# Rotary pairs on GpSimd, norm sums in two parts, high-part products first and a retention product in three float32r passes, in a two-block transformer forward pass

## The reference, cut to what matters

```python
def rmsnorm(x, g):
    y = xf * rsqrt(mean(xf * xf, -1) + 1e-6)
def apply_rope_2(x, cos, sin):            # attention of the second model, heads of 128
    x1, x2 = split(x, 2, -1)
    return x * cos + concatenate([-x2, x1], -1) * sin
# retention, per head: scores (256 queries x 512 keys), with decay, times v (512 keys x 512)
y = einsum('bhij,bhje->bhie', scores, vc) + (q * q_dec) @ state
```

## Time and profile before

| | before |
|---|---|
| median of 3 runs (lowest, highest) | 3224.12 us (3220.11, 3224.12) |
| the profiled execution | 3224.9 us, its span 3223.1 us |
| PE busy | 3185.1 us, 99% of the span |
| PE weight loads busy | 2734.2 us, 85% |
| DVE busy | 2377.3 us, 74% |
| ACT busy | 1337.1 us, 41% |
| POOL busy | 640.2 us, 20% |
| mean memory traffic | 157 GB/s |

### The profile page before, as it was taken

The page is one execution under the profiler, slowest core; times in us unless marked ns, Lnnn a source line. Parts: engine busy times, 40 slices in busy tenths (PEclk is TensorE's granted clock), DMA queues, the critical chain, the costliest instruction groups (busy, mean ns, idle before and its releaser), DMA issues.

```text
span 3223.1 us, 46716 instructions
## 1 busy us (share of the span) xinstructions
PE 3185.1 (99%) x17344; PEld 2734.2 (85%) x17344; DVE 2377.3 (74%) x3055; ACT 1337.1 (41%) x1907; POOL 640.2 (20%) x526
## 2 busy tenths in 40 slices
PE   8999999999999999999999999999999999999999
PEld 4888888888888888888888898799888889789988
DVE  4878957868787635455768887966888896975887
ACT  3222233212232224333536456455645446555643
POOL 2212322202321131001323230100223231100122
PEclk9999999999999999999999999999999999999999
DMA  6655524646365433334665665445666665444665
GB/s 225 206 161 171 162 59 134 206 139 190 90 196 178 136 103 88 98 105 138 197 178 167 197 182 159 125 137 144 184 193 177 196 189 164 124 138 119 195 196 150
DMA packets 783677, 507.50 MB, mean 157 GB/s; under 512 B 15108, under 2 KB 737104, under 8 KB 783504
## 3 DMA queue, kind: packets, MB, share of 16 engines
q1 hardware_dynamic: 782336, 503.51, 52.9%
q0 software_dynamic: 368, 1.38, 0.1%
q10 hardware_dynamic: 800, 0.24, 0.0%
HBM read 504.01 MB, written 1.05 MB: 157 GB/s over the span
## 4 chain that ended last, share of the span: by engine, by line
PE 54%; DVE 5%; issue 1%; ACT 1%; DVEq 0%; ACTq 0%
PE bank L673 18%; PE bank L671 10%; PE bank L675 4%; PE bank L677 4%; PE bank L676 4%; PE bank L690 2%; PE bank L692 2%; PE bank L691 2%; PE bank L670 2%; DVE wlo_all L1605 2%; PE bank L1146 1%; PE bank L1011 1%; DVE g_ps L2104 0%; PE bank L978 0%; DVE xn_two L1703 0%
## 5 line engine op out<-in xcount | busy, mean ns | idle before, releaser
L1605 DVE TENSOR_TENSOR wlo_all<-raw,whi_all 128x1024 fp32r<-128x1024 f32 (+3 forms) x768 | 1005.7, 1312 | 443.8 <-ACT whi_all L1215 441.1
L1215 ACT CAST whi_all<-raw 128x1024 fp32r<-128x1024 f32 (+3 forms) x768 | 834.6, 1091 | 1041.8 <-PE bank L677 552.3
L675 PE MATMUL bank<-xn_two,whi_all 128*128 128x512 f32 (+1 forms) x1760 | 631.6, 359 | 3.2 <-DVE xn_two L1779 3.1
L677 PE MATMUL bank<-xn_two,wlo_all 128*128 128x512 f32 (+1 forms) x1760 | 624.2, 355 | 0.0
L676 PE MATMUL bank<-xn_two,whi_all 128*128 128x512 f32 (+1 forms) x1760 | 624.0, 355 | 0.0
L673 PE MATMUL bank<-xn_two,whi_all 128*128 128x512 f32 x1540 | 549.4, 396 | 0.0
L2247 POOL CAST h_two<-silu_g 128x256 f32 (+1 forms) x176 | 210.0, 1193 | 1326.5 <-DVE silu_g L1844 759.2
L671 PE MATMUL bank<-xn_two,wlo_all 128*128 128x256 f32 x1760 | 456.0, 279 | 1.0 <-DVE xn_two L1779 0.8
L675 PEld LDWEIGHTS bank<-xn_two,whi_all 128*128 128x128 f32 x1760 | 332.8, 189 | 51.1 <-issue 4.2
L676 PEld LDWEIGHTS bank<-xn_two,whi_all 128*128 128x128 f32 x1760 | 332.9, 189 | 46.8 <-issue 0.7
L677 PEld LDWEIGHTS bank<-xn_two,wlo_all 128*128 128x128 f32 x1760 | 332.6, 189 | 46.5
(11 more groups left out here) (324 smaller groups left out, 4838.7 us busy)
## 6 DMA issues: line engine op xcount, KB each, us to landing
raw<-in_ffn_w_in SPq DMA_DIRECT2D x176, 512.0 KB, 3.8
raw<-in_w_in SPq DMA_DIRECT2D x168, 512.0 KB, 3.8
ada_w<-in_ada_w SPq DMA_DIRECT2D x128, 512.0 KB, 4.2
raw<-in_ffn_w_gate SPq DMA_DIRECT2D x88, 512.0 KB, 3.9
raw<-in_ffn_w_up SPq DMA_DIRECT2D x88, 512.0 KB, 4.2
raw<-in_ffn_w_down SPq DMA_DIRECT2D x32, 768.0 KB, 5.4
raw<-in_ret_w_in SPq DMA_DIRECT2D x48, 512.0 KB, 3.9
raw<-in_ffn_w_out SPq DMA_DIRECT2D x32, 768.0 KB, 5.2
```

The source lines that it names most:

```text
L675: pe.matmul(o, whi[s][:, k, :], hi, start=(k == 0), stop=False)
L677: return pe.matmul(o, wlo[s][:, k, :], hi, start=False, stop=(k == ks - 1))
L1215: act.copy(whi[s][:, 0:ks, :], raw[s][:, 0:ks, :]).then_inc(hi_done[s], 1)
L1605: tt(wlo[s][:, 0:ks, :], raw[s][:, 0:ks, :], whi[s][:, 0:ks, :].bitcast(F32), ALU.subtract).then_inc(lo_done[s], 1)
```

## The change

It has four parts. (1) The 12 `rope` steps of each mixer go from DVE to POOL, in the order that `mixer_order` gives, with the scaling of the keys between them where `root` stands. (2) `root_sum` multiplies by 128 columns of ones instead of one; the sums of POOL's part are issued first, then four `fill`, then the wait for ACT's square and the sums of that part. (3) In the first round behind a wide norm PE starts with the two products of chunk 0 that need only the high part, in all four slots, and the narrow norm's first round is now `across`. (4) The retention's y is made of three float32r products: `r_p` is split by ACT and DVE, the values by ACT (rounded copy) and DVE (low part, which now frees the banks); the scores move from behind slot 2 to behind slot 1 of `ret_g`. In the diff "..." stands where lines are left out.

```diff
--- before.py
+++ after.py
@@ -377,7 +377,8 @@
         r_z = at("r_z", [P, 4, SEQ], 90)
-        r_v = at("r_v", [P, 4, 512], 94)
+        rp_two = at("rp_two", [P, 2, 4, SEQ], 94, F32R)
+        rp_hi, rp_lo = rp_two[:, 0], rp_two[:, 1]
         r_g = at("r_g", [P, 4, SEQ], 102)
@@ -425,6 +426,7 @@
         a_v = [w[:, 0:AG, DC:KMAX, :] for w in w_f32]
+        rv_hi, rv_lo = [[w[:, t, DC:KMAX, :].rearrange("p c n -> p (c n)") for t in range(4)] for w in (whi_all, wlo_all)]
@@ -483,7 +485,7 @@
-        rt = {k: sem(f"ret_{k}") for k in ("qk", "kctx", "vd", "dm", "expo", "s", "p", "y", "var", "root",
+        rt = {k: sem(f"ret_{k}") for k in ("qk", "kctx", "vd", "vhi", "phi", "plo", "dm", "expo", "s", "p", "y", "var", "root",
                                            "yn", "yt", "z", "zhi", "zlo")}
@@ -524,6 +526,10 @@
             return bank[7 if a["mode"] == "fourier" else 4]
+        def stat_columns(a):
+            return bank[4][:, 0:2] if a["late"] else stat_bank(a)[:, 0:a["T"]:P]
@@ -707,7 +713,8 @@
-            def linear(name, moving, T, ready=None, across=False, last_late=False, start=0, late=None, behind=None):
+            def linear(name, moving, T, ready=None, across=False, last_late=False, start=0, late=None, behind=None,
+                       rounded=None):
@@ -718,7 +725,19 @@
                     if first and across:
-                        for k0, k1 in [(k, k + 1) for k in range(ks // 2)] + [(ks // 2, ks)]:
+                        if rounded is not None:
+                            pe.wait_ge(*rounded)
+                            for s in range(SLOTS):
+                                slot_ready(s, r)
+                                hi = moving(s, 0)[0]
+                                pe.matmul(bank[s][:, 0:tokens(s)], whi[s][:, 0, :], hi, start=True, stop=False)
+                                pe.matmul(bank[s][:, 0:tokens(s)], wlo[s][:, 0, :], hi, start=False, stop=False)
+                            for w in ready(0):
+                                pe.wait_ge(*w)
+                            for s in range(SLOTS):
+                                pe.matmul(bank[s][:, 0:tokens(s)], whi[s][:, 0, :], moving(s, 0)[1], start=False, stop=False)
+                        k_first = 0 if rounded is None else 1
+                        for k0, k1 in [(k, k + 1) for k in range(k_first, ks // 2)] + [(ks // 2, ks)]:
                             for s in range(SLOTS):
@@ -821,16 +840,18 @@
-                tiles = a["T"] // P
+                def sums(part, first):
+                    for c in range(0, a["T"], P):
+                        mm = pe.matmul(stat_bank(a)[:, c:c + P], part[:, c:c + P], ones[:], start=first and c == 0,
+                                       stop=not first and c == a["T"] - P)
+                    return mm
+                pe.wait_ge(ss_done, a["ss"] + 1)
+                sums(sumsq, True)
                 if a["n"] and a["mode"] != "fourier":
-                    fill(2 + tiles)
-                pe.wait_ge(ss_done, a["ss"] + 1)
+                    fill(4)
                 pe.wait_ge(sq_act, a["sq0"] + 1)
-                for c in range(tiles):
-                    for n, part in enumerate((sumsq, silu_g[0])):
-                        mm = pe.matmul(stat_bank(a)[:, c:c + 1], part[:, c * P:(c + 1) * P], ones[:, 0:1],
-                                       start=(n == 0), stop=(n == 1))
-                mm.then_inc(stat, 1)
+                sums(silu_g[0], False).then_inc(stat, 1)
@@ -883,8 +904,10 @@
                     late = a["norm"] if half == 0 and a["norm"]["late"] else None
+                    whole = a["T"] == 2 * SEQ and half == 0
                     linear(f"{a['tag']}gu{half}", moving, a["T"], ready if half == 0 else None,
-                           a["T"] == 2 * SEQ, late is not None, late=late)
+                           late is None, late is not None, late=late,
+                           rounded=(xhi, a["norm"]["hi0"] + 2) if whole else None)
                     q0 = gu_rounds(a["f"], half)
@@ -994,7 +1017,8 @@
                     if h == 0:
-                        linear("ret_qk0", lambda s, k: pair(xn_two, tok(s))(s, k), tok, ready, True)
+                        linear("ret_qk0", lambda s, k: pair(xn_two, tok(s))(s, k), tok, ready, True,
+                               rounded=(xhi, a["norm"]["hi0"] + 2))
                     else:
@@ -1003,13 +1027,15 @@
                         slot_mm(f"ret_g{h}", 0, s, short, SEQ)
-                        if s == 2:
+                        if s == 1:
                             scores(h)
-                    pe.wait_ge(rt["p"], 4 * (h + 1))
+                    pe.wait_ge(rt["plo"], h + 1)
                     for i in range(2):
+                        c = slice(i * P, (i + 1) * P)
                         for j in range(4):
-                            mm = pe.matmul(bank[4 + i][:], r_p[:, j, i * P:(i + 1) * P], r_v[:, j, :],
-                                           start=(j == 0), stop=(j == 3))
+                            pe.matmul(bank[4 + i][:], rp_hi[:, j, c], rv_hi[j], start=(j == 0), stop=False)
+                            pe.matmul(bank[4 + i][:], rp_hi[:, j, c], rv_lo[j], start=False, stop=False)
+                            mm = pe.matmul(bank[4 + i][:], rp_lo[:, j, c], rv_hi[j], start=False, stop=(j == 3))
                         mm.then_inc(rt["y"], 1)
@@ -1297,7 +1323,7 @@
                     act.activation(rstd[:, 2:4], bank[4][:, 2:4], ACT.Sqrt, scale=1.0 / D, bias=eps[:])
-                act.activation(rstd[:, 0:tiles], stat_bank(a)[:, 0:tiles], ACT.Sqrt, scale=1.0 / D,
+                act.activation(rstd[:, 0:tiles], stat_columns(a), ACT.Sqrt, scale=1.0 / D,
                                bias=(eps_sq if a["final"] else eps)[:]).then_inc(rooted, 1)
@@ -1408,7 +1434,7 @@
                     def take_tokens(t):
-                        act.copy(r_v[:, t, :], bank[t][:]).then_inc(bank_free[t], 1)
+                        act.copy(rv_hi[t], bank[t][:]).then_inc(rt["vhi"], 1)
@@ -1427,7 +1453,12 @@
                         act.activation(r_g[:, s, :], bank[s][:, 0:SEQ], ACT.Silu).then_inc(bank_free[s], 1)
-                    stream(f"ret_g{h}", gate)
+                    def round_scores(it, s):
+                        if s == 1:
+                            act.wait_ge(rt["p"], 4 * (h + 1))
+                            act.copy(rp_hi[:], r_p[:]).then_inc(rt["phi"], 1)
+                    stream(f"ret_g{h}", gate, behind=round_scores)
                     act.wait_ge(rt["var"], h + 1)
@@ -1937,15 +1968,21 @@
                     link(tt(r_m[:], r_m[:], r_p[:], ALU.add))
-                    stream(f"ret_v{h}", None, True)
+                    def low_values(it, s):
+                        for t in {2: (0, 1, 2), 3: (3,)}.get(s, ()):
+                            dve.wait_ge(rt["vhi"], 4 * h + t + 1)
+                            tt(rv_lo[t], bank[t][:], rv_hi[t].bitcast(F32), ALU.subtract).then_inc(bank_free[t], 1)
+                    stream(f"ret_v{h}", None, True, behind=low_values)
                     link.after()
                     def take_scores(it, s):
-                        if s == 2:
+                        if s == 1:
                             for j in range(4):
...
                                     ALU.mult).then_inc(rt["p"], 1)
+                            dve.wait_ge(rt["phi"], h + 1)
+                            tt(rp_lo[:], r_p[:], rp_hi[:].bitcast(F32), ALU.subtract).then_inc(rt["plo"], 1)
                     stream(f"ret_g{h}", None, True, behind=take_scores)
@@ -2010,24 +2047,6 @@
                     dve.reciprocal(dst, dst).then_inc(att["rr"], 1)
-                cos = rope2[:, 0, :].unsqueeze(1)
-                def rope(i):
-                    n, two = 12 * l + i, a_qk[:, 2 * i:2 * i + 2, :]
-                    dve.wait_ge(att["tr"], n + 1)
-                    if i:
-                        dve.wait_ge(att["rope"], n)
-                    turned = a_s[:, 0:512].rearrange("p (c t) -> p c t", c=2)
-                    for lo_, hi_ in ((0, 64), (64, 128)):
-                        other = slice(64 - lo_, 128 - lo_)
-                        link(tt(turned[lo_:hi_], a_qk[other, 2 * i:2 * i + 2, :],
-                                rope2[other, 1, :].unsqueeze(1).broadcast_to([64, 2, SEQ]), ALU.mult))
-                    link.after()
-                    link(tt(two, two, cos.broadcast_to([P, 2, SEQ]), ALU.mult))
-                    link.after()
-                    tt(two, two, turned, ALU.add).then_inc(att["rope"], 1)
@@ -2143,7 +2162,7 @@
-                steps_ = dict(unit=unit, root=root_, rope=rope, maxima=maxima, probs=probs, attended=attended,
+                steps_ = dict(unit=unit, root=root_, maxima=maxima, probs=probs, attended=attended,
                               keys=keys, decay=decay, totals=totals, keep=keep, hroot=hroot,
@@ -2270,12 +2289,42 @@
```

(26 more changed lines are left out.)

## The result

The kernel after takes 3247.99 us (median of 4 runs, 3242.76 to 3248.24), against 3224.12 us for the kernel before (4 runs, 3220.11 to 3225.34): ratio 1.0071, 95% interval 1.0055 to 1.0087. It is slower, as forecast, by 0.7% where 0.4% was forecast: 3238 us in a range of 3204 to 3258. The profiled execution takes 3248.24 us, its span 3246.4 us.

What follows compares the result with a forecast made beforehand. PE, busy 99% of the span, was taken as the bound, with DVE close to full in the mixers. Gains of 18.3 us and a rotary loss of 32 made +13.7 on 3224.9, median 3238 us; range 3204 to 3258.

Steps and rivals of the forecast that it cites:

- the third rival: Mixers: each meeting costs DVE all of POOL's instruction, 1.16 us; 3253 us in all, or 3256; chance 0.11.
- Retention y: Retention, four heads: 24 float32r instructions, one every 0.229 us, replace 16 slower ones per head; -5.5 us.
- Both covers: Retention: work on PE hides the wait for `plo` and the later release of banks; taken at 0, +8 at most.
- Norm sums: Norms: fewer sums left behind ACT's square; -0.75 us in each of three wide norms, -0.4 in the narrow; -2.7.
- clock: Wide norms: the half-clock stretches in two of them go; -3.6 us, bounds 0 and -3.6.
- High parts first: Behind the wide norms: idle time before the first product shrinks, at most 3.1 us in four waits; -3.5 with clock back.
- Narrow norm: Slot 0 behind the narrow norm: taken across four slots, its stalls for chunks go; -3.0 us.
- Rotary pairs: Mixers: rotary steps on POOL delay DVE and so PE; 16 us per mixer, +32 us for two.
- Meetings: Levels of the mixers: rotary POOL instructions that meet a DVE instruction with two SBUF inputs; 22 per mixer, +18.7 us.
- Price: Mixers: what one meeting costs DVE, 0.73 to 1.16 us, taken as 0.85 from the scalings of keys.
- Credit: Mixers: DVE, rid of its rotary steps, is earlier at `decay`; 0.6 us in seven levels, -4 per mixer.
- Clock: Mixers: one more stretch at 1.2 GHz; +1.5 us per mixer.

Runs made afterwards that it cites:

- Experiments 9 and 10: Kernel after, rotary steps on DVE; 9: norm sums of 128 columns in the old order, 3210.29 us; 10: norm sums whole as before, 3212.46 us.
- the memset run: Kernel before, rotary steps left on DVE, plus 48 dummy memsets per mixer on POOL that nobody reads: 3224.64 us, ratio 1.0000.
- experiments 5 to 7: Kernel before, rotary steps left on DVE, plus 48 POOL dummies per mixer: products 3277.54 us, copies 3241.02, memsets 3224.64.
- experiment 1: Kernel after with its twelve rotary steps per mixer back on DVE, the other three parts kept: 3207.93 us, ratio to before 0.9950.
- Experiment 12: Kernel after plus 8 unread matmuls ahead of the second half of the pairs, into the bank of the turn before the last: 3239.34 us.
- experiment 11: Kernel after plus 8 unread matmuls ahead of the second half of the pairs, behind a wait for ACT's copy of the last turn: 3251.65 us.
- 2, only the steps moved: Kernel before with only the rotary steps moved to POOL: 3263.33 us, ratio to before 1.0126.
- experiment 3: Kernel after with rotary steps 0 to 6 back on DVE and steps 7 to 11 left on POOL: 3211.44 us, ratio to before 0.9963.

## Why the prediction was right, and which terms were not

**The sign and the mechanism** were right: the gains of the other parts came, and the mixers lost more than twice as much. The two halves were each too kind: gains 15.1 us for 18.3, loss 40.1 for 32. Together that is 11.3 us, less 1.1 by which the before of that job is below 3224.12: 3248 in place of 3238. The measured time lies between the forecast and the third rival's 3253, and nearer to the rival's. That it fell into the range is owed to the width taken for that rival.

None of the three other parts was run by itself but the sums; their shares are read from the weight loads.

**Retention y, forecast -5.5.** -5.6 by the weight loads (1.36 + 2.81 + 1.40), at 0.228 us a matmul. Both covers held: no wait for `plo` or a slot is among PE's waits.

**Norm sums, clock and high parts, forecast -2.7, -3.6 and -3.5.** The second and third norms gained 4.05 and 3.33 us, as their shares of the three terms say (3.6 and 3.0). The fourth gained 0.79 for 1.3. Experiments 9 and 10 put the first term at 2.7 and the first two together at 3.5 to 5, for 6.3. High parts first was not run by itself; its wait fell from 3.1 to 1.0 us. Its largest single wait, 1.3 us, stood in the first norm (52 us). What that is worth no two traces tell, as kernels of the same code differ there by up to 2.3 us; on average the nine with the new order of products are 1.2 us ahead of the five with the old one.

**Narrow norm, forecast -3.0** and 0.4 from its sums: -3.24.

Without the first norm these sum to 17.0 us in the profile, and with it to some 18, but runs show 15.1. Half of the gap is a term that the forecast did not have, because it read the clock from one profile: that of before happens to have no stretch in the norm near 1715 us, and 12 of the 13 other kernels of this study have one, the memset run with the same code up to there among them; between before and after it makes 1.5 us. The rest stays open; it is of the size in which the runs of one kernel differ.

**Rotary pairs, forecast +18.7 - 4 + 1.5 per mixer.** *Meetings:* 22 forecast, 25 and 26 counted. *Price:* 0.85 taken, 1.06 measured. The prediction took the mixer's own rows, but those were scalings of keys; a meeting is priced by POOL's own instruction (experiments 5 to 7), which for a rotary one lasts 1.28 us. The third rival (a meeting costs all of POOL's instruction) had the mechanism and, with 1.16 from POOL's share of an addition, nearly the price. In the first mixer DVE's instructions beside rotary ones are 22.8 us longer and those beside keys alone 2.5; the keys made 4.7 before. That is 20.6 more, for 18.7. *Credit:* against experiment 1, PE's waits of `pairs` and `cross` rose by 37.5 - 11.2 = 26.3 us over two mixers, 13.1 each; so DVE's slack and relief took 7.5 in place of 4. The net of meetings and credit was foretold as 14.7, and is 13.1: that this net came out nearly right is luck, as one error covers the other.

*Clock:* this is the term that was mis-sized. 1.5 us per mixer were added for one more stretch, though level 4 of the kernel before had been 2.7 us longer for 1.6 us of meetings. Against experiment 1 the first mixer has 20.4 us at half clock for 3.4, the second 13.6 for 3.4. Half of the difference is what PE, were it busy throughout, would lose: 8.5 and 5.1 us. Waits and clock then give 26.3 + 13.6 = 39.9, and 39.0 to 40.1 were measured. Experiment 12 shows that the clock's part is real: 6.4 us came back in the mixers, net of the fills. The same account fits the mixers of the other kernels. Waits are those of `pairs` and `cross` behind DVE, in experiment 11 also those of the fills; the sum is less the 14.9 us of before; the last column is what the weight loads lose against before over both mixers, all in us.

| kernel | waits | half of the time at 1.2 GHz | fills | sum over before | loads later by |
|---|---|---|---|---|---|
| before | 11.5 | 3.4 | | 0 | 0 |
| after | 37.5 | 17.0 | | 39.6 | 39.0 |
| 1, steps on DVE | 11.2 | 3.4 | | -0.3 | 0.5 |
| 2, only the steps moved | 40.4 | 11.9 | | 37.4 | 36.9 |
| 3, steps 7 to 11 | 14.9 | 3.4 | | 3.4 | 4.2 |
| 5, products | 50.5 | 20.4 | | 56.0 | 53.8 |
| 6, copies | 24.9 | 3.4 | | 13.4 | 14.8 |
| 7, memsets | 11.6 | 3.4 | | 0.1 | 0.0 |
| 11, fills | 26.9 | 0 | 26.3 | 38.3 | 39.2 |
| 12, fills without a wait | 17.9 | 5.1 | 25.0 | 33.1 | 32.6 |

The two last columns agree within 2.2 us in all of them. Without the clock's column the kernel after would be 13 us short, that with products 15.

**POOL's deadline** was hidden, as forecast. **The levels** took 15.5 to 21.4 us, outside the forecast 17 to 20 at both ends: the level without POOL was shorter than before, the one with 20.5 us of POOL longer.

## What to carry to other kernels

Price an instruction on POOL that reads SBUF at its own length when it runs alone (here less 0.2 us) for every DVE instruction with two SBUF inputs that it meets, and not by the row of another instruction; then ask which of these stand on the path: in the levels PE felt 13 of 21 us per mixer as waits, behind them none. An engine that is given steps out of a written order runs ahead of it unless something holds it back (experiment 3). And where PE begins to wait a little in many places, add the half clock to the waits; here it was a third of the loss. Work without use in the waits, placed so that it waits for nothing itself, gave part of it back (experiment 12); with a wait of its own it gave nothing (experiment 11).

## What the runs showed of the hardware that was not expected

A POOL copy with one SBUF input delays DVE's two-input instructions just as a product does (0.41 us for a copy of 0.60 us), a memset not at all. The norms lose their clock in other places from kernel to kernel while their code stays the same: one to three stretches where the norms are those of the kernel before. Runs of one kernel differ too, and their times with them. Among nine of the kernel before in one job the three with a mean granted clock of 0.998 take 3222.5 to 3222.7 us and the three with 0.996 take 3225.1 to 3228.4; of the four of the kernel after the one with 0.996 takes 3242.76 us and the others, with 0.993 and 0.994, some 3248. The Trainium skill (TensorE: Matmul & The Clock Gate, section "What's actually happening") says that the number of matmuls at the low clock at a kernel's start differs from run to run of one kernel. These runs agree in kind, by the mean clock of a whole run. What decides which norm is hit was not tried.
